# Moving sample-attention work earlier in a one-core decoder step: page products, range reductions and value loads in another order

## The reference

```python
z = x @ w_in                                   # q, k, v, u and two gates; x is 264 rows
attn = rms_norm(attend(q, k, v, rel_bias, lam), subln_g) * (1.0 - lam_init)
ssm, s_re, s_im = s5_branch(u, ssm_re0, ssm_im0, ...)        # state-space scan, GELU, GLU
merged = gate_a * (attn @ w_proj_attn) + gate_s * (ssm @ w_proj_ssm)
h = layer_norm(alpha * x + merged @ w_out, ln1_g, ln1_b)
ffn, conv_new = conv_ffn(h, conv0, w_up, conv_w, conv_b, w_down)
y = layer_norm(alpha * h + ffn, ln2_g, ln2_b)

def sample_attention(k_past, v_past, q, k, v, rel_bias, lam):  # k_past, v_past: 16 pages of 128
    k_all = jnp.concatenate([k_past.astype(k.dtype), k], axis=1)
    v_all = jnp.concatenate([v_past.astype(v.dtype), v], axis=1)
    return diff_attention(q, k_all, v_all, q_pos, k_pos, rel_bias, lam)
```

## Time and profile before

| | us |
|---|---|
| median of three runs | 1672.56 |
| the profiled execution | 1672.43 |
| its span, first to last instruction | 1670.6 |
| PE busy | 1633.0 (98%) |
| DVE busy | 1119.0 (67%) |
| ACT busy | 650.8 (39%) |
| POOL busy | 390.4 (23%) |

### The profile page before, as it was taken

How to read it: one execution, slowest core, us unless ns; L and a number is a source line. 1 busy time by engine, 2 the same in 40 slices (tenths; PEclk the granted TensorE clock), 3 DMA queues, 4 the chain that set the end, 5 groups by cost and what they waited for, 6 DMA issues and landing times. The chain is left out here.

```text
span 1670.6 us, 31242 instructions
## 1 busy us (share of the span) xinstructions
PE 1633.0 (98%) x11730; PEld 1460.1 (87%) x11730; DVE 1119.0 (67%) x1748; ACT 650.8 (39%) x981; POOL 390.4 (23%) x341
## 2 busy tenths in 40 slices
PE   9999999999999999999998999999999999999996
PEld 7878777777677777899988999999999999999995
DVE  2383877888878944776668677776777675555555
ACT  2121344443343323333447444444444443333333
POOL 1066677787687620000000000000000000000001
PEclk9999999999999999999998999999999999999998
DMA  9669799999999979666663766766667766666651
GB/s 253 208 222 329 262 378 395 395 394 401 379 364 397 385 264 274 174 184 180 177 176 105 196 170 164 201 177 185 169 175 190 189 177 163 179 177 183 182 152 53
DMA packets 472151, 391.81 MB, mean 235 GB/s; under 512 B 23550, under 2 KB 436123, under 8 KB 472028
## 3 DMA queue, kind: packets, MB, share of 16 engines
q1 hardware_dynamic: 401388, 323.27, 62.8%
q10 hardware_dynamic: 70656, 67.11, 12.4%
HBM read 385.24 MB, written 5.46 MB: 234 GB/s over the span
## 5 line engine op out<-in xcount | busy, mean ns | idle before, releaser
L745 PE MATMUL bank<-work,weight_ring 128*128 128x264 f32 x2176 | 513.8, 390 | 1.3 <-DMA weight_ring<-in_w_in 0.8
L1509 ACT ACTIVATE weights_hi<-weight_ring 128x2048 fp32r<-128x2048 f32 (+1 forms) x166 | 309.8, 1866 | 509.6 <-PE bank L1098 389.7
L745 PEld LDWEIGHTS bank<-work,weight_ring 128*128 128x128 f32 x2176 | 403.5, 190 | 82.6 <-issue 16.7
L1978 DVE TENSOR_TENSOR weights_lo<-weight_ring,weights_hi 128x2048 fp32r<-128x2048 f32 (+1 forms) x166 | 369.1, 2224 | 111.9 <-ACT weights_hi L1509 69.6
L653 POOL TENSOR_TENSOR work<-work 128x512 f32<-128x512 f32 x256 | 319.2, 1276 | 103.4 <-DMA work<-in_cache_k 82.2
L1097 PE MATMUL bank<-h_hi,weights_hi 128*128 128x264 f32 x1344 | 330.9, 285 | 0.0
L1098 PE MATMUL bank<-h_lo,weights_hi 128*128 128x264 f32 x1344 | 330.2, 284 | 0.0
L683 POOL TENSOR_TENSOR work<-work,ffn_scratch 128x1056 f32<-128x1056 f32 x4 | 9.5, 2408 | 1046.7 <-ACT ffn_scratch L1222 1046.7
L1097 PEld LDWEIGHTS bank<-h_hi,weights_hi 128*128 128x128 f32 x1344 | 253.3, 188 | 0.0
L1098 PEld LDWEIGHTS bank<-h_lo,weights_hi 128*128 128x128 f32 x1344 | 253.0, 188 | 0.0
L1811 DVE TENSOR_REDUCE work<-work 128x8 f32<-128x512 f32 x256 | 163.2, 676 | 30.3 <-POOL work L653 30.3
(11 more groups left out here) (274 smaller groups left out, 1896.3 us busy)
## 6 DMA issues: line engine op xcount, KB each, us to landing
weight_ring<-in_w_up SPq DMA_DIRECT2D x86, 1024.0 KB, 5.7
work<-in_cache_k SPq DMA_DIRECT2D x128, 512.0 KB, 7.9
work<-in_cache_v SPq DMA_DIRECT2D x128, 512.0 KB, 7.5
weight_ring<-in_w_in ACTq DMA_DIRECT2D x60, 1024.0 KB, 15.3
weight_ring<-in_w_down SPq DMA_DIRECT2D x32, 1024.0 KB, 5.9
weight_ring<-in_w_out SPq DMA_DIRECT2D x16, 1024.0 KB, 6.0
weight_ring<-in_w_down SPq DMA_DIRECT2D x16, 704.0 KB, 4.9
weight_ring<-in_w_proj_attn SPq DMA_DIRECT2D x16, 512.0 KB, 4.3
```

The source lines that it names most:

```text
L745: last = pe.matmul(bank[(n + m) % 2][:, 0:N], chunk_weight(g, k - c * per, m), tiles[k], start=(k == 0), stop=(k == len(tiles) - 1))
L1509: act.activation(w_hi[:, (j % 2) * KT * P:(j % 2) * KT * P + k_tiles * P].bitcast(F32R), slot3(j, 0, k_tiles).rearrange("p k m -> p (k m)" ...
L1978: dve.tensor_tensor(w_lo[:, cols].bitcast(F32R), slot3(off % SLOTS, 0, k_tiles).rearrange("p k m -> p (k m)"), w_hi[:, cols], ALU.subtract ...
```

## The change

Five edits, all of order; no instruction is added or removed.

```diff
@@ SP, rounds 0 to 6: order of loads
-                for what in ("Sk", "P14", "P15", "K5", "Sv", "V0", "V1", "K6", "K7", "V2", "V3", "Bias", "K8", "Q", "V4", "K9",
+                for what in ("Sk", "P14", "P15", "V0", "K5", "V1", "K6", "Sv", "V2", "K7", "V3", "Bias", "K8", "Q", "V4", "K9",
@@ POOL, in the loop over the pages p of a round
+                    if p == 8 and i + 2 < HT:
+                        fractions(4 * i + 8)
                     if p == 11 and i + 2 < HT:
-                        fractions(4 * i + 8)
-                    if p == 14 and i + 2 < HT:
                         fractions(4 * i + 9)
@@ PE, setup: the bias of the new tokens in one piece instead of two
-            z_group((("q", 2), ("q", 3)), {3: bias_rows, 5: lambda: new_bias(0), 7: lambda: new_bias(B // 2)})
+            z_group((("q", 2), ("q", 3)), {3: bias_rows})
@@ PE, rounds 0 to 6
-                at = {2: lambda: values_to_rows(i),
+                at = {2: lambda: (values_to_rows(i), pages_pv(i - 1, 12, 13)),
                       3: lambda: max_rows(i),
-                      4: lambda: (scores(i, 1, 1), pages_pv(i - 1, 12, 13)),
-                      5: lambda: global_max(i),
-                      8: lambda: (pages_pv(i - 1, 14, 15), outputs_and_inputs(t, 0)),
+                      4: lambda: scores(i, 1, 1),
+                      5: lambda: (global_max(i), pages_pv(i - 1, 14, 15)),
+                      8: lambda: outputs_and_inputs(t, 0),
@@ ACT, rounds 0 to 6
+                if i:
+                    combined(i - 1)
                 final_states(4 * t + 2)
                 if t + 1 < HT:
                     turns(4 * t + 4)
-                if i:
-                    combined(i - 1)
                 exps(i, 0)
```

More of the change, by code:

```diff
@@ L774, in _ @@
             z_group((("q", 0), ("q", 1)), {1: lambda: x_columns(2), 2: lambda: x_columns(3), 4: lambda: x_copied(KT)})
-            rel = small[0:NB + 1, 32:32 + H]
             def bias_rows():
                 pe.wait_ge(tab_in, 32)
+                rel = small[0:NB + 1, 32:32 + H]
                 pe.matmul(bank[4][0:H, 0:384], rel, table[:, OH_TOEP:OH_TOEP + 384], start=True, stop=True).then_inc(tr, 1)
@@ L784, in bias_rows @@
                 last.then_inc(tr, 1)
-            def new_bias(b0):
-                for b in range(b0, b0 + B // 2):
+                for b in range(B):
                     last = pe.matmul(bank[6][:, b * H:(b + 1) * H], table[:, OH_NEW + b * P:OH_NEW + (b + 1) * P],
                                      rel, start=True, stop=True)
-                if b0:
-                    last.then_inc(tr, 1)
-            z_group((("q", 2), ("q", 3)), {3: bias_rows, 5: lambda: new_bias(0), 7: lambda: new_bias(B // 2)})
+                last.then_inc(tr, 1)
+            z_group((("q", 2), ("q", 3)), {3: bias_rows})
             def first_states():
```

## The result

The changed kernel takes 1685.59 us in the median of 12 runs, the kernel before 1673.3 in 12 runs. Their ratio is 1.0063, with a 95% interval of 1.0046 to 1.008: slower by 10.5 us (7.7 to 13.4). The forecast was slower by 5.9, 1678.5 us, with a range of 1671 to 1685. The timed median lies 0.6 us above that range; the ratio on the 1672.56 us that the forecast started from gives 1683.1, inside it.

What follows compares the result with a forecast made beforehand. PE, busy 98% of the span, was taken as the bound, so only its waits count. A loss of 8.4 us less a gain of 2.5 gave 5.9 on 1672.43, 1678.3, stated as 1678.5; range 1671 to 1685.

Steps and rivals of the forecast that it cites:

- part 1: `fractions` earlier on POOL, `combined` first on ACT: POOL pauses, page 15 ends 4.2 us later, PE loses 8.4 us.
- part (a): Largest score: `all_max` on DVE comes 4.2 us later, so PE waits 0.3 to 2.2 us at `global_max`.
- Part (b): Value pages 14 and 15, wanted right behind `global_max`: P15 lands at 365.3, PE waits 1.0 us, up to 1.8.
- larger loss: Rival: late key loads bunch with weights, value pages also late, 2.5 to 3.5 us more per round; 1684 to 1692, chance 0.13.
- Part 2: Value loads and products earlier: shorter waits of PE for late value pages, 2.5 us of gain, bounds 0 and 3.8.
- Part 3: Bias products in one piece in the setup: no effect, at most 0.3 us either way.
- The slack holds: Rival: P15 lands in time, only the `global_max` waits remain, 1.5 to 6 us less 2.5 to 3.8; 1670.5 to 1675, chance 0.23.
- a gain: Rival: POOL's spare time takes up the delay and the waits for values vanish; 1668.6 to 1670.5, chance 0.09.
- the long form: `differences` on DVE always slow beside POOL's unbroken work, which would make the loss 9.6 us instead of 8.4.

Runs made afterwards that it cites:

- e5: Kernel before with only `fractions` moved to pages 8 and 11 on POOL, ACT's order left as it was: 1676.4 us, ratio 1.0016.
- e6: Kernel before with only `combined` put ahead of `turns` on ACT: 1673.41 us, ratio 1.0006.
- e2: Kernel before with `fractions` at pages 8 and 11 and `combined` ahead of `turns`, nothing else: 1687.68 us, ratio 1.0082.
- e3: Kernel before with only the value loads earlier on SP and the value products earlier on PE: 1670.62 us, ratio 0.9979.
- e4: Changed kernel with the bias products apart again, as before; all the other edits kept: 1680.27 us, ratio 1.0043 to the kernel before.
- e10: Kernel before with value loads and products earlier, `combined` first, and `fractions` one page earlier, at pages 10 and 13: 1671.26 us, ratio 0.9984.
- e1: Kernel before with only the bias in one piece, `new_bias` right behind `bias_rows`: 1675.26 us, ratio 1.0003.
- e7: Kernel before with value loads and products earlier and `combined` first; `fractions` left at pages 11 and 14: 1670.61 us, ratio 0.999.
- e8: Kernel before with value loads and products earlier and `fractions` at pages 8 and 11; ACT's old order: 1671.26 us, ratio 0.9992.
- e12: Kernel before with half of `new_bias` right behind `bias_rows`, the other half at quarter 7: 1675.37 us in one run.
- e11: Kernel before with all of `new_bias` in one piece behind quarter 5, away from `bias_rows`: 1675.63 us in one run.
- e9: Kernel before with `fractions` at pages 8 and 11, `combined` first and value loads earlier; value products in their old places: 1692.39 us, ratio 1.0108.

## Why the prediction was right or wrong

**The direction and the mechanism were right.** The third `fractions` waited 12.07 us for ACT (forecast about 10) and started 0.76 us behind the start of `combined` (forecast within 1). Page 15 ended 2.3 to 3.2 us after the next round's begin (forecast about 3.4), where it ended 0.5 to 1.1 before it: 3.0 to 4.0 later, forecast 4.2. V15 landed 15.2 us after round 3's begin; the forecast's 365.3 is 15.4 on that count. e5 and e6 show that both edits are needed, which is the chain that part 1 laid out. The size was too low: 10.5 us is 1.8 times the forecast 5.9.

**Part 1 as a sum.** New waits of PE at `global_max` and at pages 14 and 15, in the profiled execution: 1.33 us in round 2 (forecast 1.4), 1.24 in round 3 (1.4), 1.12 in round 4 (2.1), 0.78 in round 5 (1.4), 0.34 in round 6 (2.1), 4.8 instead of 8.4. For part (a) the account closes. In round 4 `global_max` had 2.0 us of slack; page 15 is 3.0 later and not 4.2, and the way from `page_max` to `all_max` takes 11.0 us instead of 11.4: a wait of 0.6, measured 0.46. In round 3 page 15 is 4.0 later and that way grows from 9.75 to 11.0: 3.9 - 4.0 - 1.2 gives 1.3, measured 1.24. DVE does the same instructions on it in both, four sums of the next pages among them. What is longer is the first two of `page_max`, 0.76 and 1.23 us instead of 0.42 and 0.17; POOL no longer pauses there. The second of them before:

```profile
350.20 0.17 DVE L1818 COPY work<-work 128x16 f32<-128x16 f32 x1
```

So two premises were off: one delay for all rounds, and a way of fixed length between `page_max` and `all_max`. Part (b) gave 0.79 and 0.66 in rounds 2 and 4 (forecast 1.0) and nothing in the others.

**Part 1 as a price** was too low all the same. Alone, the two edits cost 13.7 us (e2; 10.5 to 16.9), against 8.4 with an upper bound of 13. What the sum left out is the waits for pages 4 to 7 of values, 8.6 us of waits for values in e2's profile instead of 3.8; the reading that the delayed key loads go out beside them was the rival of the larger loss, and it is argued, not shown by a run of its own. Left out too is that the clock can fall beside a wait of PE, 1.7 us each time, and that DVE can be held in `page_max`, 3.9 us in e2's profile.

**Part 2.** The forecast was 2.5 us of gain; alone it is 3.5 (1.7 to 5.2) by e3, right in kind. Within the change its value is e2 less e4, 0.0039 of the time or 6.5 us: with its interval 2.5 to 10.6; it also takes up part of what the pause costs. In the profiled execution the waits for pages 5 and 7 only shrank from 3.8 us to 1.9. Page 13, which part 2 called nearly even, made no wait in this execution, but waits of 1.99 and 2.3 us in e4's, each with a fall of the clock. Missed here: with no wait at all PE's round takes 61.37 us in e3 and e10, not 61.05. The same products have other neighbours now, and at three places of the round that takes 0.1 us more; in six rounds it is 1.9 us.

**Part 3** was the step that failed in kind: "Nothing; at most 0.3 us either way". It was weighed by when its results are used, and not by what a stretch of small products does to the clock. In the profile round 0 began at 170.73 instead of 168.75, 2.0 of the 8.0 us; against the mean of the twelve profiles without the single stretch it is 2.9, and 4.9 in e1. How much of the timed 10.5 it is stays open: e4's ratio is 0.002 under that of the change (3.3 us; with both intervals, give or take 3.7), e1's own is 0.0003.

**The account of the profiled execution:** new waits 4.8, less 1.9 of relief, the products' new neighbours 1.9, setup 2.0. That is 6.8 of 9.45 us at the end of z. Of the rest, 0.73 is a wait for ACT in round 6; what is left I have not placed. The forecast 5.9 was near the 8.0 of this execution, but that was in part luck: terms too large and terms left out made up for each other. The timed median lies 5.2 above this execution, and the two halves of the runs (1686.4 and 1681.0) put a difference of that size beside the clock; what lowered it in those runs no profile of this kernel shows. e4's profile, 1683.39 us, has what may stand there: two falls in the rounds and 8.1 us of waits for values instead of 3.4.

**The rivals.** "The slack holds" and "a gain" are out: page 15 had no slack. "A larger loss" (0.13) is nearest to what e2 shows, and in the change the earlier values bought about half of it back. Its 1684 to 1692 us hold the timed median. The stated range leaves out seven of those eight us, not half of them.

**The rule on DVE beside GpSimd.** `differences` took 3.0 us in each of rounds 1 to 5 after, where it was 2.2 to 4.2 before, and its last instruction 0.85: not the long form of 4.1 and 1.36 that the forecast expected by the rule. The Trainium skill (SBUF — State Buffer, "Who interferes with whom") lets the second to start block until the first is done. e5's 6.88 us agree with the direction, and go further: DVE's instruction was held over several POOL instructions in a row, not over one. The 0.75 us that it took at other turns beside the same stream do not go with that.

The lowest ratio found is e3's, values earlier and nothing else, 0.9979 of before; the intervals of e7 (0.999), e8 (0.9992) and e10 (0.9984) overlap with its own.

## What to carry to other kernels

Moving a producer later on one engine and its consumer earlier on another are two cheap edits that can make one dear one: work out when the result is ready and when it is asked for with both in place, and look whether the consumer has waits behind it that pay for the pause. Loads moved ahead in a queue must have their places freed as early, or they hold up all that stands behind them. And a wait of the matrix engine, like a stretch of tiny products, has to be priced with the clock that may fall beside it.

## What the runs showed of the hardware

- In a stretch of 3.5 us of small products (changed kernel and e1) the granted clock fell to 0.50 for 6.8 us. Beside shorter ones (2.2 us in e12; 1.9 us in e11, 3.8 us away from the next) it stayed at 1.00.
- Of PE's 22 waits of 1.4 to 3.7 us, 10 have a fall of 3.4 us (once 6.8) beside them. Waits of 2.75 us did not have one, one of 1.28 us (e5) did. 16 float32 product instructions took 5.49 us over such a fall (e2), and 3.83 without.
- One DVE instruction with two SBUF inputs, 0.42 us by itself, took 4.43 to 6.89 us four times while POOL ran products back to back, and 0.75 to 1.54 at other such turns.
- A small copy on DVE (128x16) took 1.23 us where POOL ran on without a pause (changed kernel, round 3) and 0.17 where it paused (before).
- A load of 512 KB took 3.1 to 12.8 us to land in e9 and 3.2 to 12.7 in the kernel before.
